# Hybrid layer with a mixture of experts: the down weights of the later experts are issued by ScalarE on its own DMA queue

## What is computed

```python
scores = jax.nn.sigmoid(t @ w_router)             # 512 tokens, 64 experts
# top 8 experts of each token, at most 4 of 8 groups; gw: their weights
def expert_block(args):
    tok, g, e = args
    xb = t_pad[tok]
    hid = jax.nn.silu(xb @ w_gate[e]) * (xb @ w_up[e])     # 1024 -> 256
    return (hid @ w_down[e]) * g[:, None]                  # 256 -> 1024
out = routed + shared
```

## Time and profile before

| | us |
|---|---|
| median of 3 runs (1232.57 to 1234.25) | 1233.0 |
| the profiled execution's own time | 1236.22 |
| its span in the trace | 1234.4 |
| TensorE busy, share of the span | 1099.9, 89% |
| ScalarE busy, share of the span | 220.9, 18% |
| mean granted TensorE clock | 0.952 |

### The profile page before, as it was taken

The page is one execution under the profiler, slowest core; times in us unless marked ns, Lnnn a source line. Parts: engine busy times, 40 slices in busy tenths (PEclk is TensorE's granted clock), DMA queues, the critical chain, the costliest instruction groups (busy, mean ns, idle before and its releaser), DMA issues.

```text
span 1234.4 us, 13233 instructions
## 1 busy us (share of the span) xinstructions
PE 1099.9 (89%) x5027; PEld 529.9 (43%) x5027; DVE 400.5 (32%) x927; ACT 220.9 (18%) x481; POOL 146.9 (12%) x194
## 2 busy tenths in 40 slices
PE   5999797888799978999699999899899998999845
PEld 3444585654444453444343433233244333433312
DVE  1784565453212022029612222122122121222137
ACT  3211422343202032031011111011111111111111
POOL 3000005020000000000212121121121221221100
PEclk9999798988899998999899999899899998999979
DMA  6225322310126320324569999999999999999577
GB/s 200 69 91 113 65 103 44 110 66 29 36 111 254 116 97 1 101 68 179 231 251 414 422 419 422 417 411 414 412 404 403 414 400 405 409 379 393 226 320 319
DMA packets 75806, 300.53 MB, mean 243 GB/s; under 512 B 20725, under 2 KB 24090, under 8 KB 50138
## 3 DMA queue, kind: packets, MB, share of 16 engines
q1 hardware_dynamic: 63066, 265.01, 55.4%
q0 software_dynamic: 12672, 34.62, 7.2%
HBM read 282.03 MB, written 27.53 MB: 251 GB/s over the span
## 4 chain that ended last, share of the span: by engine, by line
PE 81%; DVE 7%; DMA 5%; ACT 3%; issue 3%; SPq 0%; POOL 0%; POOLq 0%; DVEq 0%
PE ps L1095 26%; PE ps L707 25%; PE ps L1111 13%; PE ps L1077 4%; PE ps L831 2%; PE ps L844 2%; DMA ring<-expert_rows 2%; PE ps L983 1%; PE ps L959 1%; PE ps L1119 1%; DMA z<-in_g_final 1%; PE ps L688 1%; DVE z L1758 1%; PE ps L875 1%; DMA dw<-in_wv_x 1%
## 5 line engine op out<-in xcount | busy, mean ns | idle before, releaser
L1095 PE MATMUL ps<-ring,z 128*32 128x512 f32 (+2 forms) x1056 | 292.6, 613 | 8.7 <-issue 7.5
L707 PE MATMUL ps<-dw,act_t 128*128 128x512 f32 x576 | 250.1, 595 | 4.7 <-issue 3.8
L707 PEld LDWEIGHTS ps<-dw,act_t 128*128 128x128 f32 x576 | 109.5, 191 | 141.2 <-issue 140.1
L1111 PE MATMUL ps<-ring,act_t 128*32 128x512 f32 (+2 forms) x528 | 145.3, 596 | 0.8 <-DVE act_t L1997 0.8
L1095 PEld LDWEIGHTS ps<-ring,z 128*32 128x32 f32 (+2 forms) x1056 | 92.6, 135 | 122.2 <-issue 120.2
L1095 PE MATMUL ps<-dw,z 128*64 128x512 f32 (+2 forms) x256 | 101.1, 604 | 6.2 <-issue 5.9
L1095 PE MATMUL ps<-z 128*32 128x512 f32 (+2 forms) x288 | 86.9, 618 | 7.2 <-issue 7.2
L1436 ACT ACTIVATE tok<-ps 128x256 f32<-128x256 f32 x44 | 16.9, 383 | 329.5 <-PE ps L1095 329.5
L1955 DVE COPY z<-ps 128x512 f32<-128x512 f32 x44 | 30.4, 692 | 109.0 <-PE ps L1111 109.0
L1990 DVE SCALAR_TENSOR_TENSOR tok<-tok,gcb,ps 128x256 f32<-128x256 f32 x22 | 10.6, 481 | 169.3 <-ACT tok L1436 169.3
L2103 POOL COPY ixb<-tabs 128x1 uint32<-128x1 uint32 x88 | 16.6, 189 | 405.8 <-DVE z L1955 388.5
(11 more groups left out here) (304 smaller groups left out, 1238.4 us busy)
## 6 DMA issues: line engine op xcount, KB each, us to landing
ring<-in_w_gate SPq DMA_DIRECT2D x42, 1024.0 KB
ring<-in_w_up SPq DMA_DIRECT2D x42, 1024.0 KB
ring<-in_w_down SPq DMA_DIRECT2D x42, 1024.0 KB, 30.1
ring<-expert_rows SPq DMA_DIRECT2D x8, 2048.0 KB, 21.9
dw<-in_w_gate SPq DMA_DIRECT2D x11, 1024.0 KB
dw<-in_w_up SPq DMA_DIRECT2D x11, 1024.0 KB
act_t<-in_w_down SPq DMA_DIRECT2D x11, 1024.0 KB
z<-in_w_gate SPq DMA_DIRECT2D x11, 1024.0 KB
```

Of the source, the lines that this page charges most:

```text
L707: ins = pe.matmul(ps[0:m, bank0 + j, 0:n], lhs(w, q * 4 + c4, c4, j), rhs(w, q * 4 + c4, c4, j), start=(q == 0 and c4 == 0), stop=(q == le ...
L1095: ins = pe.matmul(ps[rows, 2 + r % 2, :], xtt[r % 2][:, c, rows], ring_wgu(BUF[x])[:, :, c, :], start=(c == 0), stop=(c == NC_D - 1))
L1111: ins = pe.matmul(ps[rows, 5 + n, :], htt[r % 2][:, c, rows], ring_wd(BUF[x])[:, c, n * 512:(n + 1) * 512], start=(c == 0), stop=(c == 1))
```

## The change

The 58 later down loads leave SyncE's program and stand in ScalarE's, behind its copy of the down bank of the round that frees the buffer. The wait for `e_y` that stood before them on SyncE goes; on ScalarE the copy has waited for it already. The reading of the expert's number (`expert_at`) now takes the engine as an argument and is done by ScalarE for these loads. Experts 0 to 3, 8 and 11, the gate and up loads, and the fallback for crowded experts (`needs_passes`) stay as they are.

```diff
+    def expert_at(eng, x):
+
+        return eng.value_load(eid[0:1, expert_column(x):expert_column(x) + 1], min_val=0, max_val=NE - 1)
+
...
         for r in range(NR + 1):
             gate_up_free = [x for x in NEXT_LOADS if LAST_ROUND[BEFORE[x]] == r]
-            down_free = [x for x in NEXT_LOADS if LAST_ROUND[BEFORE[x]] == r - 1]
             if gate_up_free:
                 sp.wait_ge(e_gu, r + 1)
             for x in gate_up_free:
-                load_gate_up(sp, expert_at(x), BUF[x])
-            if down_free:
-                sp.wait_ge(e_y, r)
-            for x in down_free:
-                load_down(sp, expert_at(x), BUF[x])
+                load_gate_up(sp, expert_at(sp, x), BUF[x])
...
             if r:
                 down_out(r - 1, (r - 1) % 4)
+                for x in NEXT_LOADS:
+                    if LAST_ROUND[BEFORE[x]] == r - 1:
+                        load_down(act, expert_at(act, x), BUF[x])
```

More of the change, by code:

```diff
@@ L625, in _ @@
         sp.dma_start(tvd, tvs).then_inc(s_tg, 16)
-        def expert_at(x):
-            return sp.value_load(eid[0:1, expert_column(x):expert_column(x) + 1], min_val=0, max_val=NE - 1)
         early, late_one = FIRST_LOADS
@@ L633, in _ @@
         sp.wait_ge(s_sh, 4)
-        load_expert(sp, expert_at(early), BUF[early])
+        load_expert(sp, expert_at(sp, early), BUF[early])
         sp.wait_ge(s_tab, 2)
         sp.wait_ge(s_tg, 16 * (NT + 2))
-        load_gate_up(sp, expert_at(late_one), BUF[late_one])
+        load_gate_up(sp, expert_at(sp, late_one), BUF[late_one])
         sp.wait_ge(s_shd, 8)
-        load_down(sp, expert_at(late_one), BUF[late_one])
+        load_down(sp, expert_at(sp, late_one), BUF[late_one])
         for r in range(NR + 1):
             gate_up_free = [x for x in NEXT_LOADS if LAST_ROUND[BEFORE[x]] == r]
-            down_free = [x for x in NEXT_LOADS if LAST_ROUND[BEFORE[x]] == r - 1]
             if gate_up_free:
```

## The result

| | before | changed |
|---|---|---|
| median of 9 runs each, us | 1234.17 (1226.65 to 1236.74) | 1244.8 (1238.36 to 1247.43) |
| ratio, with its 95% interval | | 1.0075 [1.0056, 1.0093] |
| the profiled execution's own time, us | 1236.22 | 1244.8 |
| its span, us | 1234.4 | 1243.0 |

The changed kernel is slower by 0.75%, 9.3 us at the median of before (interval 7 to 11.5). The transfers in all these kernels are issued by SyncE, GpSimd and, where the change puts them there, ScalarE; TensorE and VectorE issue none.

A forecast was written before the change was run, and what follows sets the result against it. Bound by the transfers, TensorE just under them. 1236.2 + 9.4 (order of transfers) + 1.2 (slow products) = 1246.8 us for the profiled execution, 3.2 less for the median: 1243.7 stated, the forecast's own range 1239 to 1248, chance 0.76.

The forecast's parts named there:

- The bound: Rounds: transfers bind, with TensorE's work just under them; TensorE waits 21.9 us for weights, and gate and up come last.
- SyncE: SyncE loses 58 issues, number readings and waits for down products; worth 0 as long as its queue is not empty.
- ScalarE: ScalarE gains up to two readings and issues a round, 2.2 us, covered by 6.84 us idle before its SiLU: price 0.
- The order of the transfers: Down loads on a second queue land in some 6 to 10 us instead of 30, delaying gate and up: 9.4 us.
- (a): Each gate or up load is passed by about 3.2 down loads of 2.57 us: 8.3 us later, once.
- (b): End of the stage: the last byte becomes gate and up, with 15.5 us of work behind it: 10.4 us later.
- the signs: Expected in the new profile: down loads landing after 6 to 12 us, holes before gate and up of 30 us or more.
- The 1.2 us for slow products: Last round: half a chance of 2.5 us of slow products after a long wait before the last gate and up products.
- Gathers and scatters: Sharing with two queues, they land some 5 us later at most, with rounds to spare: price 0.
- No change: Rival: the hardware queues share what generates or holds descriptors, so load order stays; 1233 us (1231 to 1235), chance 0.10.
- Faster: Rival: the down hole goes and SyncE issues gate and up sooner; at most 5.1 us, say 3.5: 1229.5 us, chance 0.08.
- ScalarE held: Rival: ScalarE's issues wait behind SyncE's full queue, costing 17 rounds x 1 us on top of the shift: 1261 us, chance 0.06.

The follow-up runs named there:

- e2: Against the changed kernel: only the first 46 down loads (experts before 52) issued by ScalarE, the last 12 by SyncE; ratio to before 1.0003, rounds 557.7 us.
- e3: Against the changed kernel: ScalarE only reads the 58 expert numbers, all down loads stay on SyncE; ratio to before 1.0001, rounds 559.2 us.
- e8: Against the changed kernel: gate and up loads of the 58 later experts also issued by ScalarE, all on one queue; ratio to before 1.0063, rounds 565.3 us.
- e7: Against the changed kernel: only the down loads of experts 62 and 63 issued by ScalarE, the other 56 by SyncE; ratio to before 1.0053, rounds 562.9 us.
- e1: Against the changed kernel: only the down loads of the last four experts issued by ScalarE, the other 54 by SyncE; ratio to before 1.0078, rounds 566.8 us.
- e5: Against the changed kernel: ScalarE issues the down loads of the last four experts one round later; ratio to before 1.0019, rounds 562.3 us.

## Why the prediction was right

**The bound** was read rightly: full engines, and gate and up as what comes last. e2 also shows that the holes in the middle are no loss by themselves. The sum of holes, 28.1 us where I said 30 or more, measures the time only together with the slow products behind them.

**SyncE** was costed at 0, and nothing speaks against it. But I said that its issues would still be held over 2 us each, and that was wrong. Its issues of up loads into `ring` (least, median and longest in ns), before and then in the changed kernel:

```profile
L530 SPq DMA_DIRECT2D ring<-in_w_up x42: 355/2083/4920, 366.3 to 1128.7; - x42
L530 SPq DMA_DIRECT2D ring<-in_w_up x42: 337/422/5220, 364.1 to 1132.2; - x42
```

The up loads fell from 2.08 to 0.42 us, the gate loads from 0.52 to 0.33. With a third fewer loads on its queue SyncE is held less often, though the longest hold, 5.22 us, is no shorter.

**ScalarE** at 0: right, by e3, e2 and its idle time of 6.83 us before the SiLU (6.84 before). Held by SyncE's full queue it was not: 0.34 us per issue. Held by its own full queue, in e8, it costs 7.8 us, not my "20 to 100": I had overlooked that the turned tokens are not needed until the down products are done.

**The order of the transfers**: right. The increase in the forecast was 10.6 us (9.4 + 1.2); measured are 9.3 by the ratio and 10.6 between the two medians. The shift of the last gate and up matrices was put at 8.3 us by (a) and 10.4 us by (b) and measured 9.9 in the profile. Down loads into `ring` land after 10.6 us, just over the 6 to 10 that I named in the sum and within the 6 to 12 of the signs.

**Some of the closeness is luck.** I took the middle of two estimates and added half of a third term, the slow products. The 1.2 us for slow products rested on one long hole before the last products. None came: the late stream shows as holes of 3.61 and 2.48 us, and the 1.7 us of slow products behind the last one are found in e3 too, where nothing was moved. Estimate (a) also counts a passing load as 2.57 us, the time of its megabyte alone, where the prediction had found 3.1 us per load in this stage, gathers and scatters included; with 3.1 it gives 10.0. And the time in the queue did not grow by either figure: up loads into `ring` land after 34.8 us in the changed kernel and after 32.0 in e7, where 56 of the 58 down loads are SyncE's (the profile of before has no figure for them). The rows don't say where the rest of the 9.9 us arises.

**Estimate (b) is the one that the runs bear out.** It said that the last byte stays where it is and changes its kind. In the changed kernel it does (552 us into the rounds in both), and in e1 as well (551), though the hole there stands a round earlier, before round 42, with 31 us of work behind it. The last gate and up products of e1 begin just after its last byte, at 551.3, and with the 15.5 us behind them that is the 566.8 measured. In e5 the last byte is again at 551 but is of a down matrix, and the gate and up matrices are there by 545.2. What (b) doesn't give is a loss where only some of the last loads overtake, as in e7. A passed load costs where a wait on it has no slack and no later wait takes it up: two overtaking loads cost 6.5 us (e7), four 9.6 (e1), 58 cost 9.3, and the first 46 alone nothing (e2).

**The premise of full engines** held to 1080 us; then the share fell to 0.91 for 48 us (0.98 before). The last byte came at 552 us all the same.

**Gathers and scatters**: about 2.3 us longer, priced at 0 with up to 5 us of growth; no wait for them appears in the chain. Right.

**The rivals.** "No change" rested on two hardware queues being one behind the engines, which the Trainium skill, page "DMA: Bandwidth & Descriptors", section "Issuing engines are not separate DMA queues", could be read to say. They do share the 16 engines and nothing was gained in bandwidth (411 GB/s from 648 to 1080 us, before 412), so far the trace agrees. But its conclusion, that issuing from a second engine saves issue time and nothing else, leaves out the order, and the order is worth 0.75% here. "Faster" did not come: its mechanism, SyncE less held, was there, and won nothing that can be seen. (Its sum named the last four holes and added the last three.) "ScalarE held" did not come in this kernel.

## What to carry to other kernels

A second DMA queue can be a way past the first one: here a load that was moved to it landed after 10.6 us instead of 30.1, and with the engines full the loads that it passed near the end came up to 9.9 us later. Before moving a load, ask which of the loads in the long queue is due soonest. Here TensorE needed them nearly in the order in which they stood: overtaking gained nothing anywhere and lost at the end. Loss in the middle of a long bound stage may be given back (e2); look for it at the last waits, where nothing follows to take it up.

## What the runs showed of the hardware that I had not expected

- How long an engine is held at its issues went with what stood on its own queue: SyncE's up issues into `ring` fell from 2.08 to 0.42 us median when the down loads left, though the 16 engines were as full.
- A nearly empty hardware queue landed 1 MB loads in 10.6 us beside a full one (ScalarE's in the changed kernel), where the same loads at the end of the full one took 30.1 us.
- With ScalarE held before 23 of its copies (100.6 us), TensorE waited 24.0 us for it in nine places (e8), and the kernel lost 7.8 us.
